# Moving the last quarter of a token projection from the latent attention into the recurrences' sweep

## The chip, the cores and the metric

One core of one Trainium2 chip runs the whole program in one launch. The metric is the device time in microseconds (us). Three runs of the kernel before gave 1419.28, 1420.89 and 1421.36 us, so the median is 1420.89 us. The profiled execution is a fourth one.

## The reference, cut to what matters

Two layers over a sequence of 512 tokens with 1024 features. In each layer the normalised input is projected once by `W_in`; three mixers read the columns; their outputs are joined and projected back.

```python
for l in range(DEPTH):                                    # DEPTH = 2
    n = rms_norm(h, norm_mix[l])
    (a_q_lat, a_kv_lat, a_k_rope, b_q, b_k, b_v, b_gate_lr, b_r,
     c_q, c_f, c_i, c_g) = jnp.split(n @ w_in[l], split_points, axis=-1)
    y_a = mla_mixer(...)      # latent attention, 4 heads, block-causal, softmax over up to 512 keys
    y_b = gla_mixer(...)      # gated recurrence, 4 heads, key width 32
    y_c = hgrn2_mixer(...)    # gated recurrence, 4 heads, key width 64; c_i are its values, c_g its gate
    h = h + jnp.concatenate([y_a, y_b, y_c], axis=-1) @ w_mix_out[l]
    h = h + memory_cross_attention(rms_norm(h, norm_ca[l]), ...)
    h = h + conv_glu_ffn(rms_norm(h, norm_ffn[l]), ...)
```

Both recurrences are `S_t = diag(decay_t) S_(t-1) + k_t v_t^T`, `o_t = S_t^T q_t`. The kernel computes the part inside a block of 128 tokens as a triangular matrix of scores.

## The kernel before, in words

**Number format.** Large products keep fp32 accuracy by splitting each operand in a high and a low part (`x_hi`, `x_lo`, `w_hi`, `w_lo`), with three matmuls for each product (`product`, lines 639, 641 and 643). The weights come in slabs of 128x1024: SP loads a slab in one of three `raw` buffers, ACT rounds it to `w_hi` (line 1173), POOL subtracts to get `w_lo` (line 565). The slabs have one order in the whole program, three buffers at each stage, and each engine takes them at places written out by hand (`ahead(name)` on ACT, the loop over `slabs` on POOL).

**The stage of the change.** All engines run programs written out by hand in order, held together by semaphores.

1. The third token projection (`cig`: columns `c_i` and `c_g` of `W_in`) has 8 chunks k of 128 features, each for 4 tiles of 128 tokens. It is cut in 16 units: one unit is one k for two token tiles, thus six 512-column matmuls. Its results are in PSUM banks 4 to 7. It is PE's filler inside the latent attention. A quarter of it is one slab: `cig 3` is k = 6 and 7, the units 12 to 15.
2. The latent attention (`attend`) works through 12 items (4 heads x 3 groups of query tiles). At step i, PE does the scores of item i, the transposes of the probabilities of item i-3 (line 801), after every third item the product with the values (PV, line 813), and then the units that `CIG_UNITS` gives to the step. DVE takes the maximum of item i and then divides the probabilities of item i-1 (line 1654). ACT evacuates the transposes (line 1229), computes the exponentials (line 1216), rounds the head's result (`ya_hi`, line 1245), and between them fills `Qx` for level 0 (`expand`, line 1253). In steps 3 and 7 the unit is interleaved with small products for the diagonals (line 921). There are steps 0 to 15; the last four have no scores.
3. The sweep of the recurrences has six levels (m = 2, 4, ... 64), each with a part x = 0 (`g`) and a part x = 1 (`h`). For a level, DVE multiplies Q by a decay (`next_queries`, line 1831), ACT copies it into the buffer `Qx` (`expand`, 4 copies per part), PE multiplies it with K (line 982; banks 0 to 3, two for each part), DVE copies the masked result into the scores (line 1860), and POOL multiplies K by a decay for the next level (line 518). `Qx` has two buffers for each part, used in turn. Where PE has done a level's matmuls it does `SWEEP_UNITS[level]` mix units: one mix unit is three matmuls of the output projection of the attention's result, on banks 4 to 7. Before the sweep's first mix unit on a bank, ACT must have emptied the bank of the `cig` result (`recurrent_values`, lines 1418 and 1419).
4. After the sweep come the transposes of K (line 993) and the states and outputs (lines 1002 to 1022).

The second `Qx` buffers lie in memory on `x_hi` and `x_lo` of k = 4 to 7. So POOL can clear them (line 512) only when all of `cig` is done, and level 1 can be expanded only behind that.

Of the kernel before, what the change touches and what calls it, by code (L numbers as in the profile page):

```python
# [27 lines left out]
def build_trunk(nc, A, out):  # L28
# [11 lines left out]
    P = 128  # L40
    DEPTH, D, P_IN = A["w_in"].shape
    SEQ = A["x"].shape[1]
# [3 lines left out]
    NH = 4  # L46
# [144 lines left out]
    with ExitStack() as ctx:  # L191
# [63 lines left out]
        ya_hi, ya_lo = place("ya_hi", R3 + 4, [P, NH, SEQ], f32r), place("ya_lo", R3 + 12, [P, NH, SEQ], f32r)  # L255
        yb_hi, yb_lo = place("yb_hi", R1 + 8, [P, NH, SEQ], f32r), place("yb_lo", R1 + 16, [P, NH, SEQ], f32r)

        Qx = [[place(f"Qx{x}_{i}", kb, [P, NH, SEQ]) for i, kb in enumerate((16 * x, 16 * x + 8))] for x in range(2)]
        qk = place("qk", R3 + 14, [P, 3, SEQ])
        decay_x = place("decay_x", R3 + 20, [P, 3, SEQ // 2])  # L260
        o_tok = place("o_tok", R1, [P, NT, 512])
        k_hat = place("k_hat", R1 + 8, [P, 3, NT, P])
        state = place("state", R1 + 14, [P, NT - 1, 512])
# [10 lines left out]
        m_hi, m_lo = place("m_hi", R1, [P, KD, NM], f32r), place("m_lo", R5 + 4, [P, KD, NM], f32r)  # L274
        ckv_tok = place("ckv_tok", R2, [P, MT, D])
        ckv_sq = place("ckv_sq", R3, [P, MT, NH, P])
        ckT = place("ckT", R3 + 4, [P, NH, NM])
        cq_tok = place("cq_tok", R3 + 8, [P, NT, NH * P])
        cqT = place("cqT", R3 + 16, [P, NH, SEQ])
# [91 lines left out]
        CIG_UNITS = {1: 4, **{i: 1 for i in range(3, 15)}}  # L371
# [3 lines left out]
        SWEEP_UNITS = (2, 1, 1, 1, 1, 2)  # L375
# [35 lines left out]
        with nc.Block() as block:  # L411
# [94 lines left out]
            def recurrences(pool, layer):  # L506

                pool.wait_ge(S["score_mm"], past(layer, "score_mm") + MLA_ITEMS)
                pool.memset(state[:, :, :], 0.0).then_inc(S["zeroed"], 1)
                pool.wait_ge(S["tok_mm"], past(layer, "tok_mm") + 2 * NT)  # L510
                for x in range(2):
                    pool.memset(Qx[x][1][:, :, :], 0.0).then_inc(S["zeroed"], 1)
                for li, m in enumerate(LEVELS):
                    for x, f in enumerate((slice(0, 1), slice(1, 3))):
# [4 lines left out]
                                           ).then_inc(S["k_level"], 1)  # L519
                pool.wait_ge(S["sg_done"], past(layer, "sg_done") + 1)  # L520
# [7 lines left out]
            def _(pool):  # L528
# [27 lines left out]
                for layer in range(DEPTH):  # L556
                    for i, (nk, cols, _) in enumerate(slabs):
# [35 lines left out]
                        if i == slab_at["cig", 3]:  # L593
                            pair_products(pool, layer)
                            score_bases(pool, layer)
                        if i == slab_at["mix", 0, 1]:
                            recurrences(pool, layer)
# [7 lines left out]
            def _(pe):  # L605
# [12 lines left out]
                for layer in range(DEPTH):  # L618
# [347 lines left out]
                    for li, m in enumerate(LEVELS):  # L966
                        for x in range(2):
                            pe.wait_ge(S["qx_done"], past(layer, "qx_done") + 2 * li + x + 1)
                            pe.wait_ge(S["k_level"], past(layer, "k_level") + 2 * li + x + 1)
                            for n in range(NT):  # L970
# [13 lines left out]
                                if n % 2:  # L984
                                    mark(mm, S["sweep_mm"])
                                    freed[b] = (S["swept"], past(layer, "swept") + 4 * li + b + 1)
                        mix_units(SWEEP_UNITS[li])

# [154 lines left out]
            def _(act_):  # L1143
# [20 lines left out]
                for layer in range(DEPTH):  # L1164
# [227 lines left out]
                    def attention_between(i):  # L1392
# [9 lines left out]
                        if i == 11:  # L1402
                            ahead(("cig", 3))
# [17 lines left out]
                    recurrent_values((0, 1))  # L1421
                    for li, m in enumerate(LEVELS):
# [9 lines left out]
                        if li == 0:  # L1432
                            recurrent_values((2, 3))
                        if li == 1:
                            ahead(("mix", 0, 0))
# [116 lines left out]
            def _(dve):  # L1552
# [50 lines left out]
                for layer in range(DEPTH):  # L1603
# [242 lines left out]

                    for li, m in enumerate(LEVELS):
                        dve.wait_ge(S["decays_done"], past(layer, "decays_done") + li + 2)
                        for x in range(2):
                            dve.wait_ge(S["qx_done"], past(layer, "qx_done") + 2 * li + x + 1)  # L1850
                            next_queries(x, m)
                        mask = pair_mask[:, li, :].rearrange("p (c m) -> p c m", m=m).unsqueeze(1).to_broadcast([P, 2 * NH, P // (2 * m), m])
                        for x, sc in enumerate((scores_g, scores_h)):
                            if li == 0:
                                dve.wait_ge(S["scores_base"], past(layer, "scores_base") + NT * (x + 1))
                            for two in range(2):
# [3 lines left out]
                                dve.copy_predicated(odd_blocks(pair, m), mask, bank).then_inc(S["swept"], 1)  # L1860
                    dve.wait_ge(S["zeroed"], past(layer, "zeroed") + 5)
# [125 lines left out]
```

## Time and profile before

| What | Value |
|---|---|
| Runs | 1419.28, 1420.89, 1421.36 us |
| Profiled execution, its own time | 1422.59 us |
| Profiled execution, span | 1420.8 us |
| PE busy | 1399.8 us, 99% |
| PE's share of the chain that ended last | 95% |
| Stage of the change, layer 0 | 158.16 to 209.52 us |
| The same stage, layer 1 | 859.67 to 911.03 us |

The span is from the first to the last instruction. A profile row of the timeline gives start and duration in us, then engine, line, operation and tiles. A matmul's duration has its tail in it, so consecutive matmuls overlap; the pace is the distance between starts. Both layers run the same program, and the stage has the same length in both, 51.36 us.

### The profile page before, as it was taken

The numbers are of one execution on the slowest core, as the hardware profiler recorded it, in microseconds if no ns is written. First come the engines' busy times: TensorE is split into PE (matmuls) and PEld (weight loads), VectorE is DVE, ScalarE is ACT, GpSimd is POOL, SyncE is SP. The second block draws the span as 40 slices with busy tenths as digits, with TensorE's granted clock in tenths as the row PEclk, the third lists the DMA queues.
The fourth block names the chain that finished last, engine by engine and source line by source line (L and its number), as shares of the span: only waits on it lengthen the run. The fifth ranks groups of instructions, "written<-read, shape, count | busy, mean of one in ns | idle before, by whom it ended". The sixth has DMA issues, their size and how long they took to land.

```text
span 1420.8 us, 17460 instructions
## 1 busy us (share of the span) xinstructions
PE 1399.8 (99%) x6863; PEld 1148.3 (81%) x6863; DVE 765.8 (54%) x1120; ACT 622.3 (44%) x1080; POOL 668.1 (47%) x371
## 2 busy tenths in 40 slices
PE   8999989999999999999999999899999999999999
PEld 6888768887788888888888877788778888888887
DVE  5574675665776206663266555836657662166611
ACT  6747483665432222332356545735753332132321
POOL 5635663542444344444446367535334444444443
PEclk9999999999999999999999999999999999999999
DMA  6332012331333233333334220223323323333322
GB/s 181 93 96 74 16 37 84 104 118 46 88 104 104 96 95 105 90 90 104 87 90 113 75 60 15 74 62 118 89 62 101 105 89 97 98 96 98 101 88 90
DMA packets 176305, 125.67 MB, mean 88 GB/s; under 512 B 14657, under 2 KB 152672, under 8 KB 176224
## 3 DMA queue, kind: packets, MB, share of 16 engines
q1 hardware_dynamic: 175664, 124.55, 29.5%
q8 instruction: 55, 0.90, 0.3%
q14 instruction: 26, 0.21, 0.0%
q10 hardware_dynamic: 560, 0.01, 0.0%
HBM read 122.44 MB, written 2.10 MB: 88 GB/s over the span
## 4 chain that ended last, share of the span: by engine, by line
PE 95%; ACT 2%; DVE 1%; issue 1%; DMA 1%; SPq 0%; DVEq 0%
PE bank L639 28%; PE bank L643 28%; PE bank L641 27%; PE bank L813 2%; PE bank L942 1%; PE bank L943 1%; ACT Qx L1253 1%; PE bank L801 1%; PE bank L1022 1%; PE bank L982 1%; PE bank L921 1%; PE bank L1097 1%; DMA x_tok<-in_x 1%; PE bank L879 0%; PE bank L1017 0%
## 5 line engine op out<-in xcount | busy, mean ns | idle before, releaser
L565 POOL TENSOR_TENSOR w_lo<-raw,w_hi 128x1024 fp32r<-128x1024 f32 (+2 forms) x230 | 546.4, 2379 | 664.3 <-ACT w_hi L1173 662.9
L1173 ACT ACTIVATE w_hi<-raw 128x1024 fp32r<-128x1024 f32 (+3 forms) x229 | 236.5, 1034 | 330.9 <-PE bank L643 330.5
L639 PE MATMUL bank<-x_hi,w_hi 128*128 128x512 f32 x944 | 371.4, 393 | 3.3 <-issue 1.6
L643 PE MATMUL bank<-x_hi,w_lo 128*128 128x512 f32 x944 | 367.6, 389 | 0.0
L641 PE MATMUL bank<-x_lo,w_hi 128*128 128x512 f32 x944 | 367.4, 389 | 0.0
L639 PEld LDWEIGHTS bank<-x_hi,w_hi 128*128 128x128 f32 x944 | 177.2, 188 | 45.9 <-issue 6.5
L641 PEld LDWEIGHTS bank<-x_lo,w_hi 128*128 128x128 f32 x944 | 177.3, 188 | 37.8 <-issue 1.4
L643 PEld LDWEIGHTS bank<-x_hi,w_lo 128*128 128x128 f32 x944 | 177.2, 188 | 37.0
L1945 DVE SCALAR_TENSOR_TENSOR conv<-gate_in,gains_all,conv 128x512 f32<-128x512 f32 x44 | 118.2, 2685 | 1.6
L1537 ACT ACTIVATE conv_silu<-conv 128x512 f32<-128x512 f32 x44 | 27.8, 632 | 169.5 <-DVE conv L1946 169.5
L1673 DVE TENSOR_TENSOR h<-h,bank 128x512 f32<-128x512 f32 x48 | 31.8, 682 | 105.2 <-PE bank L643 105.1
L1941 DVE TENSOR_TENSOR gate_in<-bank,r_bc 128x512 f32<-128x512 f32 x44 | 30.4, 692 | 105.9 <-PE bank L643 96.3
L639 PE MATMUL bank<-w_hi,x_hi 128*128 128x512 f32 (+1 forms) x192 | 78.1, 407 | 0.0
L1606 DVE SCALAR_TENSOR_TENSOR x_lo<-h,gains_all,x_hi 128x512 fp32r<-128x512 f32 x40 | 41.9, 1058 | 64.1 <-ACT x_hi L1190 63.1
L643 PE MATMUL bank<-w_hi,x_lo 128*128 128x512 f32 (+1 forms) x192 | 75.3, 392 | 0.0
L641 PE MATMUL bank<-w_lo,x_hi 128*128 128x512 f32 (+1 forms) x192 | 74.9, 390 | 0.0
L639 PE MATMUL bank<-a_hi,w_hi 128*128 128x512 f32 x176 | 68.5, 389 | 0.0
L641 PE MATMUL bank<-a_lo,w_hi 128*128 128x512 f32 x176 | 68.5, 389 | 0.0
L643 PE MATMUL bank<-a_hi,w_lo 128*128 128x512 f32 x176 | 68.5, 389 | 0.0
L639 PE MATMUL bank<-w_hi,a_hi 128*128 128x512 f32 x176 | 68.5, 389 | 0.0
L641 PE MATMUL bank<-w_lo,a_hi 128*128 128x512 f32 x176 | 68.5, 389 | 0.0
L643 PE MATMUL bank<-w_hi,a_lo 128*128 128x512 f32 x176 | 68.5, 389 | 0.0
(318 smaller groups left out, 2273.0 us busy)
## 6 DMA issues: line engine op xcount, KB each, us to landing
raw<-in_w_ffn_in SPq DMA_DIRECT2D x88, 512.0 KB, 3.8
raw<-in_w_ffn_out SPq DMA_DIRECT2D x40, 512.0 KB, 3.6
raw<-in_w_in SPq DMA_DIRECT2D x27, 512.0 KB, 3.8
raw<-in_w_mix_out SPq DMA_DIRECT2D x16, 512.0 KB, 3.9
raw<-in_w_ca_kv SPq DMA_DIRECT2D x32, 256.0 KB, 3.2
raw<-in_w_ca_q SPq DMA_DIRECT2D x8, 512.0 KB, 3.3
raw<-in_w_ca_out SPq DMA_DIRECT2D x8, 512.0 KB, 3.9
raw<-in_w_in SPq DMA_DIRECT2D x12, 256.0 KB, 2.9
```

The costliest lines, as they stand in the source:

```text
L565: pool.tensor_tensor(w_lo[gi % SPLIT][:, c0:n], raw[gi % RAW][:, c0:n], w_hi[gi % SPLIT][:, c0:n].bitcast(f32), ALU.subtract).then_inc(S[" ...
L639: pe.matmul(o, ah, bh, start=first, stop=False)
L641: pe.matmul(o, ah, bl, start=False, stop=False)
L643: mm = pe.matmul(o, al, bh, start=False, stop=last)
L801: mm = pe.transpose(pb[b][:, c:c + P], pr[j % FLIGHT][:, c:c + P], ident[:, :])
L813: mm = pe.matmul(pb[b][:, q0:SEQ], values(n, hd), pT[hd % len(pT)][:, n, q0:SEQ], start=(n == 0), stop=(n == n_blocks - 1))
L1173: act_.activation(w_hi[k % SPLIT][:, 0:n], raw[k % RAW][:, 0:n], ACT.Copy).then_inc(S["hi_split"], 1)
L1537: act_.activation(conv_silu[n % 2][:, :], conv[n % 2][:, :], ACT.Silu).then_inc(S["silu_done"], 1)
L1606: dve.scalar_tensor_tensor(x_lo[:, k, :], h[:, k, :], gain_of(layer + w // 3, name, k), x_hi[:, k, :].bitcast(f32), ALU.mult, ALU.subtract ...
L1673: dve.tensor_tensor(h[:, k, :], h[:, k, :], pb[PROJ_BANKS[base // H_ADDS][half][c]][:, :], ALU.add).then_inc(S["h_added"], 1)
L1941: dve.tensor_tensor(gi[:, CONV - 1:], pb[4 * g + 2 * (n % 2)][:, :], r_bc[:, :], ALU.mult).then_inc(S["gate_ready"], 1)
L1945: link(dve.scalar_tensor_tensor(cv[:, :], gi[:, t:t + SEQ], w_(t), cv[:, :], ALU.mult, ALU.add))
```

## The change

The projection's last four units leave the attention's steps 8, 9, 10 and 13 and go into the sweep: two behind level 0, one behind level 1, one behind level 2. The mix units in the sweep are still eight, later distributed. So that the sweep can begin while k = 6 and 7 of `x_hi` and `x_lo` are still read, the second `Qx` buffers get homes elsewhere, and with them `ya`, `yb`, `o_tok`, `k_hat`, `state` and the operands of the cross attention. POOL clears `state` and `Qx0_1` right after the slab `mix 0,0`, and `Qx1_1` after the last transposes of probabilities. It subtracts the slab `mix 0,1` behind its K products of level 2 (before: ahead of the whole sweep). ACT rounds that slab after step 15 (before: 11), and empties the `cig` banks after levels 1 and 2. DVE takes the queries of the next level between its copies.

```diff
-        ya_hi, ya_lo = place("ya_hi", R3 + 4, [P, NH, SEQ], f32r), place("ya_lo", R3 + 12, [P, NH, SEQ], f32r)
-        yb_hi, yb_lo = place("yb_hi", R1 + 8, [P, NH, SEQ], f32r), place("yb_lo", R1 + 16, [P, NH, SEQ], f32r)
-        Qx = [[place(f"Qx{x}_{i}", kb, [P, NH, SEQ]) for i, kb in enumerate((16 * x, 16 * x + 8))] for x in range(2)]
+        ya_hi, ya_lo = place("ya_hi", R1, [P, NH, SEQ], f32r), place("ya_lo", R1 + 8, [P, NH, SEQ], f32r)
+        yb_hi, yb_lo = place("yb_hi", R3 + 8, [P, NH, SEQ], f32r), place("yb_lo", R1 + 16, [P, NH, SEQ], f32r)
+        Qx = [[place(f"Qx{x}_{i}", kb, [P, NH, SEQ]) for i, kb in enumerate((16 * x, (R3 + 4, R0 + 8)[x]))] for x in range(2)]
...
-        o_tok = place("o_tok", R1, [P, NT, 512])
-        k_hat = place("k_hat", R1 + 8, [P, 3, NT, P])
-        state = place("state", R1 + 14, [P, NT - 1, 512])
+        o_tok = place("o_tok", R3, [P, NT, 512])
+        k_hat = place("k_hat", R3 + 8, [P, 3, NT, P])
+        state = place("state", R3 + 14, [P, NT - 1, 512])
...
-        m_hi, m_lo = place("m_hi", R1, [P, KD, NM], f32r), place("m_lo", R5 + 4, [P, KD, NM], f32r)
+        m_hi, m_lo = place("m_hi", R3, [P, KD, NM], f32r), place("m_lo", R5 + 4, [P, KD, NM], f32r)
...
-        ckv_sq = place("ckv_sq", R3, [P, MT, NH, P])
-        ckT = place("ckT", R3 + 4, [P, NH, NM])
-        cq_tok = place("cq_tok", R3 + 8, [P, NT, NH * P])
-        cqT = place("cqT", R3 + 16, [P, NH, SEQ])
+        ckv_sq = place("ckv_sq", R1, [P, MT, NH, P])
+        ckT = place("ckT", R1 + 4, [P, NH, NM])
+        cq_tok = place("cq_tok", R1 + 8, [P, NT, NH * P])
+        cqT = place("cqT", R1 + 16, [P, NH, SEQ])
...
-        CIG_UNITS = {1: 4, **{i: 1 for i in range(3, 15)}}
+        CIG_UNITS = {1: 4, **{i: 1 for i in (3, 4, 5, 6, 7, 11, 12, 14)}}
+        CIG_LATE = (2, 1, 1, 0, 0, 0)
...
-        SWEEP_UNITS = (2, 1, 1, 1, 1, 2)
+        SWEEP_UNITS = (0, 0, 1, 2, 2, 3)
...
-            def recurrences(pool, layer):
-
-                pool.wait_ge(S["score_mm"], past(layer, "score_mm") + MLA_ITEMS)
+            def spare_operands(pool, layer):
+
                 pool.memset(state[:, :, :], 0.0).then_inc(S["zeroed"], 1)
-                pool.wait_ge(S["tok_mm"], past(layer, "tok_mm") + 2 * NT)
-                for x in range(2):
-                    pool.memset(Qx[x][1][:, :, :], 0.0).then_inc(S["zeroed"], 1)
-                for li, m in enumerate(LEVELS):
+                pool.memset(Qx[0][1][:, :, :], 0.0).then_inc(S["zeroed"], 1)
+                pool.wait_ge(S["probsT_mm"], past(layer, "probsT_mm") + MLA_ITEMS)
+                pool.memset(Qx[1][1][:, :, :], 0.0).then_inc(S["zeroed"], 1)
+
+            def recurrences(pool, layer, levels):
+
+                for li in levels:
+                    m = LEVELS[li]
                     for x, f in enumerate((slice(0, 1), slice(1, 3))):
                         pool.wait_ge(S["sweep_mm"], past(layer, "sweep_mm") + 4 * li + 2 * (x + 1))
                         d = block_decay(m, slice(0, P), f).rearrange("p f (b two) -> p f b two", two=2)[:, :, :, 1:2]
...
                         pool.tensor_tensor(k, k, d.to_broadcast([P, 1 + x, SEQ // (2 * m), m]), ALU.mult
                                            ).then_inc(S["k_level"], 1)
+
+            def gate_gains(pool, layer):
...
+                        if i == slab_at["mix", 0, 0]:
+                            spare_operands(pool, layer)
+                            recurrences(pool, layer, range(3))
                         if i == slab_at["mix", 0, 1]:
-                            recurrences(pool, layer)
+                            recurrences(pool, layer, range(3, len(LEVELS)))
+                            gate_gains(pool, layer)
...
                                     mark(mm, S["sweep_mm"])
                                     freed[b] = (S["swept"], past(layer, "swept") + 4 * li + b + 1)
+                        for u in range(sum(CIG_UNITS.values()) + sum(CIG_LATE[:li]), sum(CIG_UNITS.values()) + sum(CIG_LATE[:li + 1])):
+                            tok_unit("cig", 1, u // 2, (2 * (u % 2), 2 * (u % 2) + 1))
                         mix_units(SWEEP_UNITS[li])
...
-                        if i == 11:
+                        if i == 15:
                             ahead(("cig", 3))
...
-                    recurrent_values((0, 1))
                     for li, m in enumerate(LEVELS):
...
                                     expand(li + 1, x, hd)
-                        if li == 0:
-                            recurrent_values((2, 3))
-                        if li == 1:
+                        if li in (1, 2):
+                            recurrent_values((2 * li - 2, 2 * li - 1))
+                        if li == len(LEVELS) - 2:
                             ahead(("mix", 0, 0))
...
+                    def queries_of_level(li, x):
+                        dve.wait_ge(S["decays_done"], past(layer, "decays_done") + li + 2)
+                        dve.wait_ge(S["qx_done"], past(layer, "qx_done") + 2 * li + x + 1)
+                        next_queries(x, LEVELS[li])
+
+                    for x in range(2):
+                        queries_of_level(0, x)
                     for li, m in enumerate(LEVELS):
-                        dve.wait_ge(S["decays_done"], past(layer, "decays_done") + li + 2)
-                        for x in range(2):
-                            dve.wait_ge(S["qx_done"], past(layer, "qx_done") + 2 * li + x + 1)
-                            next_queries(x, m)
                         mask = pair_mask[:, li, :].rearrange("p (c m) -> p c m", m=m).unsqueeze(1).to_broadcast([P, 2 * NH, P // (2 * m), m])
...
                                 dve.copy_predicated(odd_blocks(pair, m), mask, bank).then_inc(S["swept"], 1)
+                            if li + 1 < len(LEVELS):
+                                queries_of_level(li + 1, x)
```

## Rows read from the trace of the kernel before

**Rows 1.** The page, parts 1 and 4.
```profile
PE 1399.8 (99%) x6863; PEld 1148.3 (81%) x6863; DVE 765.8 (54%) x1120; ACT 622.3 (44%) x1080; POOL 668.1 (47%) x371
...
PE 95%; ACT 2%; DVE 1%; issue 1%; DMA 1%; SPq 0%; DVEq 0%
```

**Rows 2.** Windows: length, busy us (instructions) by engine, granted clock, DMA share, GB/s.
```profile
158.16:183.33 25.17, 25.17 (x112) 17.73 (x111) 15.06 (x28) 13.69 (x32) 19.79 (x13) 1.00 0.06 21
183.33:209.52 26.19, 21.65 (x289) 16.44 (x289) 24.36 (x37) 24.72 (x53) 13.67 (x14) 1.00 0.02 2
209.52:240.00 30.48, 30.48 (x193) 27.16 (x192) 17.11 (x41) 10.55 (x23) 14.07 (x8) 1.00 0.31 104
...
884.84:911.03 26.19, 21.63 (x290) 16.44 (x290) 24.35 (x37) 24.71 (x53) 13.64 (x14) 1.00 0.02 3
```

**Rows 3.** Timeline of PE in the attention's steps 9 to 15.
```profile
165.50 0.47 PE L639 MATMUL bank<-w_hi,x_hi 128*128 128x512 f32 x1
...
166.97 0.81 PE L942 MATMUL bank<-kT_n,qT_n 128*128 128x384 f32 x2
...
168.50 0.48 PE L639 MATMUL bank<-w_hi,x_hi 128*128 128x512 f32 x1
...
173.53 0.49 PE L801 MATMUL bank<-ident,probs 128*128 128x128 f32 x3
...
175.93 0.47 PE L639 MATMUL bank<-w_hi,x_hi 128*128 128x512 f32 x1
...
181.09 2.32 PE L813 MATMUL bank<-probsT,v_tok 128*128 128x512 f32 x8
```

**Rows 4.** Timelines of DVE, of ACT and of POOL beside it.
```profile
162.88 1.89 DVE L1831 TENSOR_TENSOR Q<-Q,decay 128x512 f32<-128x512 f32 x1
...
170.47 2.54 DVE L1654 TENSOR_SCALAR probs<-probs,small 128x128 f32<-128x128 f32 x2
...
166.72 0.57 ACT L1216 ACTIVATE probs<-bank,small 128x256 f32<-128x256 f32 x1
...
174.85 1.04 ACT L1173 ACTIVATE w_hi<-raw 128x1024 fp32r<-128x1024 f32 x1
...
178.65 0.49 ACT L1229 ACTIVATE probsT<-bank 128x384 f32<-128x384 f32 x1
...
164.18 6.16 POOL L493 TENSOR_TENSOR scores_h<-pair_eye,small 128x512 f32<-128x512 f32 x4
170.30 2.35 POOL L565 TENSOR_TENSOR w_lo<-raw,w_hi 128x1024 fp32r<-128x1024 f32 x1
175.97 2.41 POOL L565 TENSOR_TENSOR w_lo<-raw,w_hi 128x1024 fp32r<-128x1024 f32 x1 [3.31 <-ACT w_hi L1173]
```

**Rows 5.** Timeline of PE in the sweep; in brackets the idle time before, with its releaser.
```profile
187.63 0.66 PE L982 MATMUL bank<-Qx,K 128*64 128x128 f32 x8 [0.53 <-DVE scores_g L1860]
...
194.67 1.15 PE L982 MATMUL bank<-Qx,K 128*64 128x64 f32 x32 [0.63 <-ACT Qx L1253]
...
197.34 1.09 PE L982 MATMUL bank<-Qx,K 128*64 128x128 f32 x16 [0.62 <-ACT Qx L1253]
```

**Rows 6.** Timelines of DVE, ACT and POOL in the sweep.
```profile
186.17 2.45 DVE L1860 COPY_PREDICATED scores_g<-pair_mask,bank 128x512 f32<-128x512 uint8 x2
...
195.61 10.32 ACT L1253 ACTIVATE Qx<-Q 32x256 f32<-32x256 f32 x24
...
202.07 1.44 DVE L1831 TENSOR_TENSOR Q<-Q,decay_x 128x256 f32<-128x256 f32 x2
...
202.19 0.76 POOL L518 TENSOR_TENSOR K<-K,decay_x 128x256 f32<-128x256 f32 x1 [0.81 <-PE bank L982]
```

**Rows 7.** Windows at the diagonals of step 3 and where the clock changed.
```profile
135.20:138.61 3.41, 3.41 (x27) 3.20 (x26) 3.30 (x9) 2.82 (x9) 1.87 (x1) 1.00 0.01 2
138.61:142.03 3.42, 3.42 (x9) 2.17 (x9) 1.07 (x1) 0.20 (x1) 0.52 (x1) 0.50 0.40 141
...
841.76:845.17 3.41, 3.41 (x11) 2.52 (x10) 2.52 (x7) 1.15 (x3) 0.00 (x0) 0.50 0.09 32
```

## The prediction

> **What bounds the kernel now.** I read the page first: PE is busy for 99% of the span and is 95% of the chain that ended last [rows 1]. So a change can gain only where PE idles, and whatever makes PE idle costs its full length. Then windows over the stage of the change. In the attention's steps 8 to 15 PE is busy for 25.17 of 25.17 us; in the sweep for 21.65 of 26.19, and layer 1 shows the same; behind the sweep there is no idle time at all [rows 2]. There are thus 4.54 us of idle PE per layer, all in the sweep, and the change moves filler into it. Whether that pays is decided by what the other engines allow in the attention once the filler is gone. For that I read the timelines of PE, DVE, ACT and POOL beside each other.
>
> What they show in the attention: PE never waits, but only since the units cover two late operands. DVE is late because of POOL. DVE's multiplication at 162.88 takes 1.89 us and ends only once POOL's operation of that time has ended; the two divisions at 170.47 take 2.54 us and end at 173.01, just behind POOL's subtraction, which started at 170.30, 0.17 us ahead of them, and ran to 172.65 [rows 4]. In the sweep, the waits are for DVE's copies at level 1 and for ACT's expansions later [rows 5]; ACT is at 24.72 and DVE at 24.36 of 26.19 us [rows 2].
>
> The sum is made against the profiled execution: 1422.59 us, span 1420.8, thus 1.8 us around it. It is 1.7 us above the median of the runs, 1420.89, to which I add the difference.
>
> **The change part by part.**
>
> *Units out of the attention.* One unit costs 166.97 - 165.50 = 1.47 us of PE's pace, four 5.88 us. Laid out from 158.16 on, the start of step 8: to 165.50 PE has scores, transposes and PV of steps 8 and 9 and one unit; without the unit it is there at 164.03. Scores 10 with transposes 7 take 168.50 - 166.97 = 1.53 us [rows 3], so PE is at 165.56. Scores 11 need the bank of scores 9, thus ACT's exponentials of item 9; the last of them starts at 166.72 [rows 4] and its result is there at about 167.4. This time doesn't move, since it hangs on DVE's stalled multiplication at 162.88. New wait: 1.85 us. Scores 11, transposes 8 and their unit take 173.53 - 168.50 - 1.47 = 3.56 us, to 171.0. Transposes 9 need the divisions that end at 173.01, and DVE reaches them no earlier, for it is held by POOL's score bases (6.16 us from 164.18) and then by the subtraction [rows 4]. New wait: 2.1 us. Transposes 9 and PV take 2.40 us (173.53 to 175.93), the unit 1.47 [rows 3], transposes 10 0.25 by their two records: 177.2. Transposes 11 need ACT's evacuation of transposes 10, which starts at 178.65 now; ACT loses the rounding of a slab (1.04 us at 174.85) ahead of it [rows 4], so it ends at about 178.1. New wait: 0.95 us. The last PV starts at 181.09 now [rows 3]; in the new order at 181.09 - 5.88 + 4.9 = 180.1. **The attention gives 0.9 to 1.0 us of the 5.88 that it loses.** Bounds: nothing of it (each wait 0.3 longer), or 3.1 if DVE slips in ahead of the subtraction (below).
>
> *Units into the sweep.* I count PE's pace without waits: the levels 2.1, three of 1.95, 1.9 and 3.6 us, eight mix units of 0.7 and a tenth at each change of kind, in all 19.5 us, so the sweep's 26.2 hold 6.7 us of waits (the windows count 4.54 because a matmul's tail covers some 0.2 us of each of ten waits). With four units the pace is 25.4 us. What waits are left, by laying the four engines' orders out with the durations of [rows 5, 6]:
> - Level 1, part x = 1: its banks wait for the copies of level 0, which come every 1.15 us (2.45 us for two) where PE needs 0.47. Now ahead of them comes DVE's multiplication for level 1. Two waits, 0.74 and 0.68 us. The waits of part x = 0 are covered by the two units behind level 0.
> - Level 2: unit 14 (1.47 us) covers it.
> - Level 3, part x = 1: POOL's subtraction of slab `mix 0,1`, 2.4 us [rows 4], now stands in the sweep, behind POOL's K products of level 2, at about 195.5. DVE's multiplication for level 3 comes 0.2 us later and is held until 197.9, as it is at 202.07, where two multiplications take 1.44 us with a K product beside them [rows 6]. The copies of level 2 for x = 1 are behind it, and PE waits for them: 1.5 us. Then PE is late enough that nothing else waits: levels 4 and 5 have two and three mix units, and ACT's expansions (0.43 us each, 40 of them, 24 take 10.32, rows 6) end at about 205.6, with the last part of level 5 at 206.7.
> - Small waits at level 0 and 3: 0.3 us.
>
> Together 3.2 us; 25.4 + 3.2 = 28.6, less the 0.3 us by which this way of laying out makes today's sweep too long (26.5 for 26.19): 28.3. **The sweep costs 28.3 - 26.2 = 2.1 us more.** Without POOL's subtraction in it the layout gives only 0.2 us less, since PE is then held by its own work and by ACT's chain at the same places. Bounds: 25.4 (no waits, -0.8) and 32.1 (all 6.7 us of waits stay, +5.9).
>
> *Everything else.* ACT's emptying of the banks (8 copies, 2.9 us) moves behind levels 1 and 2, where it delays the expansions of levels 3 and 4; it is in the layout. The mix units now need it late, and it is done over 1 us ahead of each. POOL's memsets leave the sweep: 1.8 us each, at 172.7 and after the last transposes. Whether a memset holds DVE as a subtraction does, no row shows; if it did, the divisions at 174.15 would end at about 175.9, and their user comes at 176.9, so between 0 and 0.1 us. New homes cost no instruction, and the waits on them are the old ones; 0, with no row that could bound it further than that the same operations have the same durations in both layers. SP's loads keep their order; DMA moves 2 GB/s in the sweep [rows 2], so a slab freed 20 us later has a free queue, and the slab behind `mix 0,1` waits for the end of the sweep as before. The work behind the sweep shifts as a whole, since PE has no idle time there.
>
> The Trainium skill, SBUF — State Buffer, section Who interferes with whom, says that a Vector instruction with two SBUF inputs is held by a GpSimd instruction that reads SBUF, for the whole of it, and not by one that only writes. By that the moved memsets cost nothing at all, and the moved subtraction holds DVE; the sum is the same by either.
>
> Sum per layer: -0.95 + 2.1 = +1.1 us. Two layers: +2.1 us. The profiled execution would be at 1424.7 us, the median at **1423.0 us**.
>
> **The rivals.**
>
> *The clock falls in the new gaps (slower).* In layer 0 the granted clock was 0.50 (1.2 instead of 2.4 GHz) from 138.61 to 142.03, behind the stretch of the diagonals, in which PE counts as busy for 3.41 of 3.41 us but has the small products of line 921 between a unit's matmuls; in layer 1 it stayed low twice as long, to 845.17 [rows 7]. The new gaps of 1.85 and 2.1 us with 3.6 us of work between them could be such a place, too. Against it: level 1 of the sweep has gaps as well, and the clock is 1.00 there [rows 2]. A fall of that length costs half of 3.4 us, 1.7 us, if it hits PV 2, on which everything to the sweep hangs. One fall: +3.8, 1424.7; in both layers +5.5, 1426.4.
> The Trainium skill, TensorE: Matmul & The Clock Gate, section HAM oscillation, puts the danger in idle gaps longer than any of mine; by it this rival would give nothing. The rows show a fall without an idle gap, so I keep it.
>
> *DVE gets in ahead of POOL's subtraction (faster).* Today it comes 0.17 us too late at 170.3 [rows 4]. Place: the division of item 9. If DVE is there before 170.30, it takes 0.6 us instead of 2.54; PE's wait of 2.1 us goes, and the attention ends 3.1 us earlier than now. Per layer -3.1 + 2.1 = -1.0, in all -2.0: 1418.9. For it: in the new order the PV of head 1 is earlier, and with it the subtraction `ya_lo` on DVE, by 0.1 us. Against: the small operation before the divisions is itself held by POOL's last score base until 170.34, whenever it comes.
>
> *The sweep's chain from DVE over ACT to PE grows (slower).* In the new order a multiplication for the next level can hold the copies behind it until ACT has expanded. If it does so by 0.5 us at each of five steps, it is +2.5 per layer: 1428.0. Against it: in the layout ACT is ahead of DVE at each of them, by 0.1 us at level 3 for x = 0 and by 0.5 or more elsewhere.
>
> **How the numbers follow.** My sum 50% (own range 1421.0 to 1425.0, half a us per layer and the spread of the runs, 2 us); the clock 27%; DVE ahead 12%; the chain 11%. No change that can be told is 0.2%, or 2.8 us: 1418.1 to 1423.7. Slower: nine tenths of the clock's case, all of the chain's, a quarter of my own, less a little for the spread: 0.44. Faster: a third of DVE ahead, and some for gains in the sweep down to its bound (-3.6 in all): 0.10. Between: 0.46. The range leaves out the second fall's and the chain's upper part and the lower part of the gain: 1418.8 to 1427.2.
>
> **What would show it.** Right: PE idle at about 165.6, 171.0 and 177.2 in layer 0; the last PV at 180.1; DVE's two divisions near 170.5 still with 2.5 us; two waits for copies at level 1; POOL's line 565 inside the sweep with a DVE line 1831 of about 2.4 us beside it; PE's first line 993 at about 210.6. Wrong: line 993 before 209.5, or a wait for ACT in levels 4 and 5, or another length behind the sweep, or a change of the durations of the moved operands' operations; a low clock after 171 would show the first rival.

## The result and the profile after

Four runs of the changed kernel took 1427.72, 1431.31, 1433.18 and 1433.22 us: median 1432.24 us, against 1420.64 us of the kernel before with a fourth run added (1420.39). The ratio is 1.0080, 95% interval 1.0067 to 1.0093. So the change costs 11.6 us, over five times my forecast of 2.1, and the time is outside my range. The profiled execution is the 1427.72 us one, the shortest of the four (span 1426.0; mean granted clock 0.998, the other three 0.994).

The page after, parts 1 and 4, answers to [rows 1]: PE is 2 points less of the chain, DVE 2 points more.

```profile
PE 1398.2 (98%) x6863; PEld 1147.4 (80%) x6863; DVE 771.9 (54%) x1120; ACT 622.6 (44%) x1080; POOL 668.2 (47%) x371
...
PE 93%; DVE 3%; ACT 2%; issue 1%; DMA 0%; DVEq 0%; ACTq 0%
```

Windows after (columns as in [rows 2]): two stretches round the idle time of layer 1, the attention from the last matmuls of step 8 on in layer 0, and both sweeps. They answer to [rows 2, 7].

```profile
873.54:876.95 3.41, 0.19 (x2) 0.22 (x3) 3.37 (x4) 0.00 (x0) 2.86 (x2) 1.00 0.51 154
876.95:880.36 3.41, 3.41 (x8) 1.77 (x7) 1.81 (x6) 1.63 (x4) 0.00 (x0) 0.50 0.00 0
160.10:183.72 23.62, 18.27 (x82) 12.33 (x82) 16.41 (x28) 11.71 (x29) 15.64 (x10) 1.00 0.08 22
183.72:212.04 28.32, 26.41 (x313) 20.98 (x313) 25.45 (x37) 25.83 (x54) 15.54 (x14) 1.00 0.02 6
887.87:916.17 28.30, 26.34 (x314) 20.98 (x313) 25.42 (x37) 25.80 (x54) 15.52 (x14) 1.00 0.04 8
```

The sweep takes 28.3 us in both layers, as forecast. The attention is where it went wrong: PE idles for 5.4 of 23.6 us. PE's waits in the attention, layer 0 and then layer 1 (us in total, times, longest), of which the kernel before had none:

```profile
PE bank L811 <- DVE probs L1665: 2.3, 1, 2.3
PE bank L952 <- ACT probs L1228: 2.2, 1, 2.2
PE bank L811 <- ACT probsT L1241: 0.9, 1, 0.9
...
PE bank L811 <- DVE probs L1665: 5.0, 1, 5.0
PE bank L952 <- ACT probs L1228: 1.2, 1, 1.2
PE bank L811 <- ACT probsT L1241: 0.9, 1, 0.9
```

The three places are the ones I named. But in layer 1 the wait ahead of transposes 9 is 5.0 us. What holds DVE there stands in the timelines of PE, DVE and POOL (answering to [rows 3, 4]), first layer 1, then layer 0:

```profile
876.76 0.72 PE L811 MATMUL bank<-ident,probs 128*128 128x128 f32 x3 [4.99 <-DVE probs L1665]
...
871.15 5.46 DVE L1665 TENSOR_SCALAR probs<-probs,small 128x128 f32<-128x128 f32 x2
...
870.99 2.35 POOL L571 TENSOR_TENSOR w_lo<-raw,w_hi 128x1024 fp32r<-128x1024 f32 x1
873.29 1.37 POOL L509 MEMSET state<- 128x1536 f32 x1
874.60 1.80 POOL L510 MEMSET Qx<- 128x2048 f32 x1
...
171.00 3.14 DVE L1665 TENSOR_SCALAR probs<-probs,small 128x128 f32<-128x128 f32 x2
...
168.33 2.54 POOL L571 TENSOR_TENSOR w_lo<-raw,w_hi 128x1024 fp32r<-128x1024 f32 x1
170.81 1.37 POOL L509 MEMSET state<- 128x1536 f32 x1
172.13 1.80 POOL L510 MEMSET Qx<- 128x2048 f32 x1
```

The same two divisions took 2.54 us before [rows 4]. Now they take 5.46 and end at 876.6, 0.2 us behind the second memset (874.60 + 1.80 = 876.40). In layer 0 DVE came 0.13 us after POOL's subtraction had ended (168.33 + 2.54 = 170.87) and still took 3.14 us: it was held by the memsets alone. In that layer the clock fell at 156.73, in step 8, which shifts PE and DVE against POOL, so that this profile shows the smaller of two cases. The run with the units back, below, has the same pair in the other order: 5.47 us in layer 0, and in layer 1, with a fall in step 8 (863.22), 3.15.

### The profile page after: what moved, and what is told of

It reads as the page before. It is cut to its first block, busy times and chain, and to the rows that moved or that the text cites. A ratio compares the mean times of both kernels' runs of the same rounds, so it can differ in the third digit from the quotient of the medians.

```text
span 1426.0 us, 17472 instructions
## 1 busy us (share of the span) xinstructions
PE 1398.2 (98%) x6863; PEld 1147.4 (80%) x6863; DVE 771.9 (54%) x1120; ACT 622.6 (44%) x1080; POOL 668.2 (47%) x371
## 4 chain that ended last, share of the span: by engine, by line
PE 93%; DVE 3%; ACT 2%; issue 1%; DMA 0%; DVEq 0%; ACTq 0%
PE bank L649 27%; PE bank L653 27%; PE bank L651 27%; PE bank L823 2%; PE bank L952 1%; PE bank L1034 1%; PE bank L953 1%; PE bank L992 1%; DVE probs L1665 1%; PE bank L811 1%; ACT Qx L1265 1%; DVE Q L1842 1%; PE bank L1109 1%; PE bank L931 1%; PE bank L889 0%
```

## The experiments

Each was timed beside the kernel before on one chip. Ratios are to that kernel, with 95% intervals; a run's mean granted clock is given where it matters. Theories: **A**, the two memsets right behind POOL's subtraction hold DVE's divisions. **B**, the clock falls behind PE's new gaps and makes them dearer. Rivals: the new homes, the new orders in the sweep, or the move of the units itself.

**Memsets late.**

```diff
-                pool.memset(state[:, :, :], 0.0).then_inc(S["zeroed"], 1)
-                pool.memset(Qx[0][1][:, :, :], 0.0).then_inc(S["zeroed"], 1)
                 pool.wait_ge(S["probsT_mm"], past(layer, "probsT_mm") + MLA_ITEMS)
+                pool.memset(state[:, :, :], 0.0).then_inc(S["zeroed"], 1)
+                pool.memset(Qx[0][1][:, :, :], 0.0).then_inc(S["zeroed"], 1)
                 pool.memset(Qx[1][1][:, :, :], 0.0).then_inc(S["zeroed"], 1)
```

> The changed kernel, but POOL clears state and Qx0_1 only behind its wait for the last transposes of the attention, so nothing of POOL stands behind its subtraction at 168.3 to 170.9. Theory A (the two memsets, 1.37 and 1.80 us, hold DVE's divisions behind the subtraction): the divisions at 171.0 (3.0 us) and, in layer 1, at 871.15 (5.3 us) take about 2.5 us as in the kernel before; PE's step from the work before transposes 9 to transposes 9 is idle for about 2.1 us in both layers instead of 2.65 and 5.37; the sweep stays at 28.3 us, at most 0.2 us longer; in all 1 + 3 us less, 1428 us for the median if the clock falls as often as in the changed kernel, 1424 if the long gap was what brought the falls. Theory B (the memsets are harmless, POOL's subtraction alone holds DVE and the clock does the rest): gaps and time as in the changed kernel, 1432 us.

Measured: 1422.66 us, ratio 1.0027 (1.0015 to 1.0039); the kernel before 1419.94. So by the medians the memsets' place was 8.9 of the 11.6 us (11.6 less 2.7); by the two ratios it is 7.5 (0.0080 less 0.0027), and their intervals don't meet. The time is also below the 1424 us that I had for the case that the clock no longer falls. DVE's divisions in layer 0 and PE's wait in layer 1:

```profile
168.85 2.54 DVE L1665 TENSOR_SCALAR probs<-probs,small 128x128 f32<-128x128 f32 x2
...
874.50 0.52 PE L811 MATMUL bank<-ident,probs 128*128 128x128 f32 x3 [2.05 <-DVE probs L1665]
```

The window of its sweep, layer 0:

```profile
182.66:211.05 28.39, 26.41 (x313) 20.98 (x313) 25.48 (x37) 25.84 (x54) 17.08 (x15) 1.00 0.04 10
```

The divisions are back at 2.54 us and the wait at 2.1 in both layers, just as predicted for the change itself. The sweep is the same. The twelve executions differ, though: seven at clock 0.998 to 1.000 took 1420.4 to 1423.2 us, five at 0.995 or 0.996 took 1425.6 to 1428.1. With this one edit the time would have been inside my range.

**One memset late**, the dose in between: only the line for `Qx[0][1]` moves behind the wait.

> The changed kernel with only Qx0_1's memset (1.80 us) put behind the wait for the last transposes; state's (1.37 us) stays right behind the subtraction of slab mix 0,0. Theory A as a dose: DVE's divisions of item 9 end about 1.8 us earlier than with both, PE's wait ahead of transposes 9 is 3.3 to 3.5 us in both layers (5.1 with both memsets where DVE comes behind the subtraction, 2.1 with none): 1425 to 1428 us. Rival (the length has nothing to do with what POOL does behind the subtraction): 2.1 us and 1423, or 5 us and 1432.

Measured: 1427.99 us, ratio 1.0061 (1.0047 to 1.0074). PE's wait is 3.2 us in both layers. DVE's row and POOL's two:

```profile
169.97 3.73 DVE L1665 TENSOR_SCALAR probs<-probs,small 128x128 f32<-128x128 f32 x2
...
169.79 2.37 POOL L571 TENSOR_TENSOR w_lo<-raw,w_hi 128x1024 fp32r<-128x1024 f32 x1
172.09 1.39 POOL L509 MEMSET state<- 128x1536 f32 x1
```

The divisions take 2.54 us with no memset, 3.73 with state's and 5.46 with both: each memset adds nearly its own length, 1.2 and 1.7 us (the memsets take 1.39 and 1.80). Theory A is shown for the wait, in mechanism and size. The time moves by more than the waits do: 8.2 us above the kernel before, where 2.7 and twice 1.1 us more of wait make 4.9; these four executions were at clock 0.993 to 0.996.

**Early memsets in the kernel before**, with the new homes but all units in the attention (`slab_at["mix", 0, 0]` gets the two memsets; `recurrences` keeps `Qx[1][1]`).

> The kernel before with the new homes, and of the orders only this: POOL clears state and Qx0_1 right behind its subtraction of slab mix 0,0. All 16 units stay in the attention, so PE has its filler. POOL's subtraction of mix 0,1 comes behind the memsets. Theory A: DVE's two divisions at 170.5 end no earlier than POOL's memsets at 175.8, and the second perhaps only behind the next subtraction at 178.4; transposes 9, at 173.5 in the kernel before, wait 2.4 to 4.8 us per layer: 1425 to 1430 us. Rival (a memset only writes and holds nothing, or the filler covers it): the divisions end at 173.0 as before, 1420.5 us.

Measured: 1427.13 us, ratio 1.0049 (1.0035 to 1.0063), 6.4 us above the kernel before. The rows of DVE and of POOL, and then PE's wait in the attention, alike in both layers:

```profile
171.16 5.47 DVE L1654 TENSOR_SCALAR probs<-probs,small 128x128 f32<-128x128 f32 x2
...
173.25 1.42 POOL L594 MEMSET state<- 128x1536 f32 x1
174.57 1.84 POOL L595 MEMSET Qx<- 128x2048 f32 x1
```

```profile
PE bank L801 <- DVE probs L1654: 2.4, 1, 2.4
```

Twice 2.4 us are 4.8. The other 1.6 us aren't tied to one place: the profile has a fall of the clock behind each of the two waits (at 176.82 and 879.96), and none at 138 and 838, where the kernel before had its own. The filler covered only 0.5 us of the hold.

**Homes alone**: the kernel before with the changed `place` lines.

> The kernel before with nothing but the new places of ya, yb, the second Qx buffers, o_tok, k_hat, state and the operands of the cross attention. My theory: homes cost nothing, 1420.9 us within 1.5, all stages as in the kernel before (the sweep 26.2 us, the rest behind it unchanged). Rival: new neighbours in memory change durations or waits behind the sweep, several us, seen as a longer stretch between the sweep of layer 0 and that of layer 1 (701.5 us before).

Measured: 1420.50 us, ratio 1.0000 (0.9992 to 1.0009). From sweep to sweep 701.51 us, as before. The homes cost nothing that these runs can tell (1.3 us at most).

**Units back**: `CIG_UNITS`, `SWEEP_UNITS`, ACT's emptying and its rounding inside the sweep as before, no late units, all else changed.

> The changed kernel with the projection's four units back at steps 8, 9, 10 and 13, the mix units in the sweep and ACT's emptying of the banks as before; the homes, POOL's order (early memsets, the subtraction inside the sweep), ACT's rounding after step 15 and DVE's order in the sweep stay changed. My theory: the units cover what POOL's memsets and ACT's exponentials cost, so no gap over 0.5 us in the attention of layer 0 and at most 1 us in layer 1, the sweep within 0.5 us of 26.2, 1420 to 1423 us. Rival (the new orders cost by themselves): a gap of 1 us or more ahead of transposes 9 and a sweep of 27 us or more, 1424 to 1428 us.

Measured: 1429.65 us, ratio 1.0070 (1.0057 to 1.0083). My expectation fell, the rival's came true: PE waits 2.4 us for the divisions in layer 0 and 0.7 in layer 1, and the sweep takes 28.4 us with a fall of the clock in it (at 204.45 and 907.60). The rows of PE, DVE and POOL at level 3 of that sweep:

```profile
204.62 1.98 PE L992 MATMUL bank<-Qx,K 128*64 128x64 f32 x32 [1.93 <-DVE scores_h L1875]
...
201.65 2.23 DVE L1843 TENSOR_TENSOR Q<-Q,decay_x 128x256 f32<-128x256 f32 x1 [0.75 <-ACT Qx L1265]
...
201.24 2.35 POOL L571 TENSOR_TENSOR w_lo<-raw,w_hi 128x1024 fp32r<-128x1024 f32 x1
```

This is the level 3 wait of my layout, 1.9 us long, in a kernel whose PE is not late enough to hide it. So the move of the units is not what loses most: with them back in the attention, the places of the memsets and the new orders cost 9.7 us by themselves, the falls of the clock included (0.993 to 0.996 in these runs).

**Units twice**: a unit repeated at the end of steps 10 and 11.

```diff
+                        if i in (10, 11):
+                            tok_unit("cig", 1, 4, (0, 1))
```

> The changed kernel with one unit of the projection (six matmuls, 1.47 us of PE's pace) done once more at the end of step 10 and once more at the end of step 11, in both layers, so a part of k = 4 is added three times: 5.9 us more of PE's work in all, put just where PE idles. Theory B (part of the loss is the clock, which falls behind the new gaps): the units lie in gaps of 2.2 and 2.7 to 5.4 us and cost nothing, the gaps shrink to 0.5 us and 1 to 4 us, and the falls to half clock that the changed kernel has more of than the kernel before go: median below the changed kernel's 1432, near 1427. Theory A alone (only the lengths of the gaps matter): the time stays at 1431 to 1433, since the work only fills idle time. If the gaps were not where I read them, 5.9 us more: 1438.

Measured: 1430.14 us, ratio 1.0073 (1.0059 to 1.0086). With 5.9 us more work it is no longer than the changed kernel (10.2 us above its own base for 11.6; the intervals overlap), so the added work lay in idle time. It leaves out that each part of the product may be added only once, so it doesn't compute what the reference does and only its time is of use. PE's wait ahead of transposes 9 is 3.7 us in both layers: 5.2 with the unit added, so layer 1 of the changed kernel's profile is the common case. Theory B isn't borne out the way I wrote it: the 3.7 us that were left each had a fall behind them (175.27 and 878.41), and the runs lie at clock 0.996 to 0.998. The changed kernel's longer ones lay at 0.994, so fewer falls than there are likely, but the time doesn't settle it.

**The refit**: four moves against what had been seen.

```diff
+                        if i == slab_at["mix", 0, 0]:
+                            pool.wait_ge(S["probsT_mm"], past(layer, "probsT_mm") + MLA_ITEMS - 2)
...
+                pool.wait_ge(S["probsT_mm"], past(layer, "probsT_mm") + MLA_ITEMS - 1)
                 pool.memset(state[:, :, :], 0.0).then_inc(S["zeroed"], 1)
...
-        CIG_UNITS = {1: 4, **{i: 1 for i in (3, 4, 5, 6, 7, 11, 12, 14)}}
-        CIG_LATE = (2, 1, 1, 0, 0, 0)
-        SWEEP_UNITS = (0, 0, 1, 2, 2, 3)
+        CIG_UNITS = {1: 4, **{i: 1 for i in (3, 4, 5, 6, 7, 10, 13)}, 11: 2}
+        CIG_LATE = (2, 1, 0, 0, 0, 0)
+        SWEEP_UNITS = (0, 1, 1, 2, 2, 2)
...
-                            recurrences(pool, layer, range(3))
...
-                            recurrences(pool, layer, range(3, len(LEVELS)))
+                            recurrences(pool, layer, range(len(LEVELS)))
```

> A refit of the change to what the first four runs showed. POOL: the subtraction of slab mix 0,0 behind transposes 9, state and Qx0_1 cleared behind transposes 10, Qx1_1 behind transposes 11, the subtraction of mix 0,1 ahead of the sweep again. PE: one unit back at step 10, two units at step 11, one at 13 (none at 12 and 14), so three units go into the sweep (two behind level 0, one behind level 1), mix units 0, 1, 1, 2, 2, 2. Theory A (what DVE's two-port operations lose to POOL and what the moved units no longer cover is all): PE's waits ahead of scores 11 and transposes 9 fall from 1.2 and 2.1 us (with the memsets late) to under 0.5 us each, the transposes of K start 2.0 us earlier per layer than with the memsets late alone, thus 0.5 us earlier than in the kernel before: 1418.7 us, and no fall to half clock behind steps 10 to 12. Rival (the clock falls wherever the sweep or the attention is changed): the waits go, but the time stays at 1421 to 1424.

Measured: 1418.89 us, ratio 0.9991 (0.9982 to 1.0000). The transposes of K start at 208.93 us, 0.6 earlier than in the kernel before, close to my 0.5. The ratio's interval ends at 1.0000, so a gain is barely told. The waits for exponentials 9 and divisions 9 are gone; in their place are three for ACT's evacuations (1.8 us in all).

**The refit with the subtraction in the sweep**, as the change has it.

> The refit, but POOL's subtraction of slab mix 0,1 stands in the sweep, behind its K products of level 2, as in the changed kernel. My prediction's size for it: 0.2 us per layer, because PE is held by its own work; by the layout of the refit 0.5 us, thus 1.0 us above the refit. Rival, from the run with the units back (DVE's multiplication 2.23 us beside the subtraction, PE then waits 1.93 us for the copies): 1.5 us or more per layer, 3 us or more above the refit.

Measured: 1420.86 us, ratio 1.0007 (0.9998 to 1.0016). That is 2.0 us above the refit; the sweep takes 28.51 for 27.36 us in layer 0, 1.15 us more. That lies between the 0.5 us of the layout and the rival's 1.5. My 0.2 us for this in the prediction was too small, for this layout.

**The refit with DVE's old order** in the sweep.

> The refit with DVE's old order in the sweep: both multiplications of a level ahead of all its copies. By the layout 0.65 us per layer more than the refit, as PE waits 2.5 us instead of 1.0 for the first mix unit's bank: 1.3 us above the refit. Rival (DVE's new order is itself a cost of the sweep, because a multiplication waits for ACT with copies behind it): up to 2 us below the refit.

Measured: 1422.79 us, ratio 1.0022 (1.0011 to 1.0033), 3.9 us above the refit and not 1.3. PE's wait for the first mix unit's bank is 2.5 us, as laid out. The sweep of layer 0 takes 29.37 us for the refit's 27.36, and in the profile each sweep has a fall in it (194.37 and 894.11); what a fall costs (1.4 us, below) and the 0.65 of the layout make up that difference. All its runs had lower clocks, 0.993 to 0.998 for the refit's 0.998 to 0.999. So the rival, by which the new order is itself a cost, is out; how much of the 3.9 us is its waits and how much the clock, these runs don't separate.

**The refit with the mix units early**: three units behind level 0, ACT empties all four banks there.

```diff
+        CIG_UNITS = {1: 4, **{i: 1 for i in (3, 4, 5, 6, 7, 10, 12)}, 11: 2}
+        CIG_LATE = (3, 0, 0, 0, 0, 0)
+        SWEEP_UNITS = (2, 2, 1, 1, 1, 1)
...
-                        if li in (1, 2):
-                            recurrent_values((2 * li - 2, 2 * li - 1))
+                        if li == 0:
+                            recurrent_values(range(NT))
```

> The refit once more: the second unit-free step is 13 instead of 12, all three late units stand behind level 0, ACT empties the four banks right behind its expansions for level 1, and the mix units are 2, 2, 1, 1, 1, 1. In the refit PE waited 1.1 us for the first mix unit's bank and 0.6, 0.5 and 0.2 us inside the levels. By the layout with all four engines' orders the waits of levels 1 and 2 go and the states start 2.3 us earlier per layer than in the refit: 1414.3 us. Rival (ACT is the bound of the sweep, 24.7 of 26.2 us busy in the kernel before, so emptying the banks earlier only delays the expansions of levels 2 and 3, and PE's waits move there): 1417 to 1419 us.

Measured: 1415.28 us, ratio 0.9966 (0.9954 to 0.9979), 4.5 us less than the kernel before; of all the kernels so far it is the first that is clearly faster. The time lies between my 1414.3 and the rival's 1417. The sweep holds three units more than before and takes 24.9 us in layer 1, where the kernel before took 26.2 [rows 2].

**A memset in the sweep**: as that one, with `state` cleared ahead of K's level 3.

> As the kernel before it in this set, but POOL clears state (1.37 us) inside the sweep, behind its K products of level 2, where DVE multiplies Q by the decay (two inputs in SBUF, 0.41 to 0.68 us undisturbed) and copies by mask. Theory A in its wide form (any two-port operation of DVE is held by a memset): a DVE multiplication beside the memset takes 1.3 us or more. Narrow form (a memset holds the divisions, which have one input tile and write in two-port mode, but not an operation with two SBUF inputs): the multiplication beside it keeps 0.4 to 0.7 us. The time within 1 us of the kernel before it in either case.

Measured: 1414.62 us, ratio 0.9977 (0.9963 to 0.9991); its five runs at full clock took 1413.8 to 1414.4 us, those of the kernel ahead 1413.9; four of its runs at 0.995 or 0.996 took 1419.2 to 1420.8, which is why the ratio is nearer 1 than the median. POOL's two rows and DVE's two, and then the window of the sweep:

```profile
195.35 1.38 POOL L518 MEMSET state<- 128x1536 f32 x1
196.69 1.66 POOL L524 TENSOR_TENSOR K<-K,decay_x 128x256 f32<-128x256 f32 x2
...
195.66 0.69 DVE L1845 TENSOR_TENSOR Q<-Q,decay_x 128x512 f32<-128x512 f32 x1
...
197.47 1.16 DVE L1845 TENSOR_TENSOR Q<-Q,decay_x 128x256 f32<-128x256 f32 x1
```

```profile
180.52:205.79 25.27, 24.58 (x308) 19.70 (x307) 23.79 (x37) 24.51 (x53) 15.28 (x14) 1.00 0.01 2
```

The multiplication at 195.66 runs wholly beside the memset and keeps its 0.69 us, in layer 1 (891.92) as well. The one at 197.47, beside a K product, takes 1.16 for 0.42. So the narrow form holds: a memset delays DVE's `TENSOR_SCALAR` (one tile in, one out), not its `TENSOR_TENSOR` with two inputs in memory; POOL's products delay both.

## Why the prediction was wrong

**The step that failed** is in *Everything else*: "Whether a memset holds DVE as a subtraction does, no row shows; if it did, the divisions at 174.15 would end at about 175.9 ... so between 0 and 0.1 us." The size is 2.9 us per layer (5.46 for 2.54 us of DVE, 5.0 for 2.1 us of PE's wait). Two faults lie in it. I had taken a price of both sides for the unknown, but worked it out for the wrong instruction: for the next division in DVE's order, and not for the one that [rows 4] show waiting since 170.47 behind the subtraction. That one isn't done when the subtraction ends. Taken one by one, the two divisions of layer 1 are recorded from 871.15 to 876.48 and from 873.35 to 876.61: the second's record begins as the subtraction ends, at 873.34, as it did before at 172.66, but both end only behind the second memset. And I had removed the units that stood ahead of its user, which cover 0.5 us of it in the run with early memsets in the kernel before.

The second fault is the rule I set beside it. The Trainium skill, SBUF — State Buffer, section Who interferes with whom, has two rules of this kind. I quoted the one for two SBUF inputs; the division is a `tensor_scalar`, and for that the page says that it can enter a two-port mode, which contends with GpSimd as such, and the second to issue blocks for the whole instruction. By that rule a memset can hold a division, as the subtraction does, and the runs agree with both rules: the division issued 0.19 us behind a memset took 3.14 us (171.00 for 170.81), the multiplication beside one kept its 0.69. That a division already waiting when the memsets begin is held by them too, 5.3 us over three POOL instructions, is more than the page says.

**The rest of the sum held.** Against the run with late memsets, in which only this step is taken out:

| Step | Predicted | Measured there |
|---|---|---|
| Wait ahead of scores 11 | 1.85 us | 1.2 us |
| Wait ahead of transposes 9 | 2.1 us | 2.1 us |
| Wait ahead of transposes 11 | 0.95 us | 0.9 us |
| Attention gives | 0.9 to 1.0 us | 0.8 us, a fall of the clock taken off |
| Sweep | 28.3 us | 28.4 us |
| Homes | 0 | 0.0 (0.9992 to 1.0009) |
| Both layers | +2.1 us | +2.7 us by the medians, 3.8 by the ratio (2.1 to 5.5) |

The 0.8 us are from layer 0: 26.04 us from step 8 (156.62) to the sweep (182.66), 1.7 of it a fall in PV 2 (4.01 for 2.32 us), thus 24.35 for the 25.17 of before [rows 2]. Layer 1 gives the same. The wait ahead of scores 11 is the term that was furthest off. In the prediction's last sum, -0.95 and +2.1 for each layer make 2.3 us for two and not 2.1.

Within the sweep the total was right and its parts were not. In the changed kernel's layer 0, the waits at level 1 are there (0.69 and 0.37 us; I had 0.74 and 0.68), but DVE's multiplication for level 3 started 0.13 us ahead of the subtraction (197.09 to 197.22) and escaped. The next one was held, and PE waited at level 4, 0.65 us and not 1.5. Rows of PE, DVE and POOL, answering to [rows 5, 6]:

```profile
190.60 0.69 PE L992 MATMUL bank<-Qx,K 128*64 128x64 f32 x16 [0.69 <-DVE scores_h L1874]
191.65 0.69 PE L992 MATMUL bank<-Qx,K 128*64 128x64 f32 x16 [0.37 <-DVE scores_h L1874]
...
203.63 0.58 PE L992 MATMUL bank<-Qx,K 128*32 128x64 f32 x14 [0.65 <-DVE scores_h L1874]
...
198.82 1.53 DVE L1842 TENSOR_TENSOR Q<-Q,decay_x 128x512 f32<-128x512 f32 x1
...
197.22 2.58 POOL L571 TENSOR_TENSOR w_lo<-raw,w_hi 128x1024 fp32r<-128x1024 f32 x1
```

**The first rival was half right.** The clock did fall at the place I named: in the profile at 876.95, 0.2 us behind the start of transposes 9, and PV 2 ran at 0.50. I gave it 27%, with gaps of 2 us; the real gap there was 5, but with late memsets it fell behind the 2.1 us as well (171.92 and 875.07). Over all thirteen profiles, PE's longest step from one matmul to the next ahead of transposes 9 to 11 was 2.4 us or more in eleven layers. In ten of them a fall began in that gap or up to 1.1 us behind it. In the other fifteen layers, with 0.4 to 1.2 us, none did there. But a long gap isn't needed: with the mix units early a fall began at 180.68, 0.9 us behind waits of 0.9 and 0.8 us at the attention's end, and others, as at 138.61 [rows 7], have no wait ahead of them. Nor is it certain in any one execution: the run with late memsets has 2.45 us in both layers of its profile, and two of its twelve executions had a mean clock of 1.000.

The price of a fall is an estimate from the kernel before: in the first comparison it took 1417.6 to 1418.3 us at clock 1.000 and 1422.3 to 1422.5 at 0.996, which is 11.4 us at half clock (0.004 x 1420 x 2) or 3.3 falls of 3.4 us, 1.4 us each. One execution of the same comparison doesn't fit: clock 0.988 and 1420.70 us. By that price the changed kernel's three longer runs at 0.994 had five (17 us), about 7 us. So the 11.6 us are, as far as this goes: 2.7 for the change without the memsets' place, 5.8 for the hold in two layers (2 x 2.9), and the last 3 for more falls than the kernel before. The first two terms are shown by runs; the last is what remains. The clocks would make it more: executions of the kernel before at 1420.5 to 1420.9 us had 0.998, and from there to 0.994 are 3.3 falls, 4.6 us. So the split is good to some 1.5 us. That in the unprofiled runs of the changed kernel layer 0 is held as long as layer 1 is argued from the three other profiles with both memsets early (5.5 us of DVE in layer 0 of each), not seen. ACT's later rounding of a slab was in no run undone by itself.

The rivals of DVE getting in ahead of the subtraction and of a longer chain from DVE over ACT didn't occur.

## What to carry to other kernels

Moving a GpSimd instruction next to another one can make a longer block for Vector, even if what is moved only clears memory: look at every Vector instruction that already waits there, not at those that come after. Before filler is taken from beside a late operand, ask what that operand waits for and whether the same edit lengthens it. Here filler had to stand right ahead of the two late operands; with two units put there, GpSimd's work set behind Vector's last division and the sweep's banks emptied at once, the same idea, with three units moved and not four, was worth 4.5 us.

## What the runs showed of the hardware that was not expected

A Vector `TENSOR_SCALAR` issued 0.16 us behind a GpSimd subtraction waited through it and through two memsets behind it, 5.3 us in all (871.15 to 876.48). Between POOL's four score bases it gets in, though they also follow without a gap: the division below starts beside the second of them in `scores_h` (866.73 to 868.12) and is done at 868.41, while the third runs. Rows of the changed kernel, layer 1, POOL and DVE:

```profile
864.93 6.09 POOL L494 TENSOR_TENSOR scores_h<-pair_eye,small 128x512 f32<-128x512 f32 x4
...
866.91 1.50 DVE L1665 TENSOR_SCALAR probs<-probs,small 128x512 f32<-128x512 f32 x1
```

Why the one chain shuts Vector out and the other doesn't, no run here tells apart.

PE's clock fell behind idle time of 2.1 us (with late memsets, both layers), and executions of that one kernel differ by up to 7.7 us, from 1420.36 at a mean clock of 1.000 to 1428.07 at 0.995. The Trainium skill, TensorE: Matmul & The Clock Gate, section HAM oscillation, warns of idle gaps longer than that; by it the clock would have stayed up behind the waits I had forecast, and the falls at 171.92 and 875.07 are just there. A comparison of two kernels within 1% needs its runs' granted clocks beside their times.
